# A two-block transformer kernel: gathered pairs in another order, three sets of expert weights, and tile 0's gated sum ahead of late dot products

## What is computed

```python
# block 1
mod = silu(c) @ w_ada + b_ada                  # six vectors of 1024
y = g_attn * (attn @ w_o_attn) + g_rec * (rec @ w_o_lru)      # the gated sum
x = x + gate1 * (y @ w_out)
h2 = rms_norm(x, norm2_g) * (1 + scale2) + shift2
q = (h2 @ w_query).reshape(tokens, 8 heads, 2, 128)
s = einsum('thpd,hpnd->thpn', q, sub_keys)     # two lists of 128 key scores
s_top, i_top = top_k(s, 16)                    # then the 16 best of 16 x 16 sums
idx, g = ...                                   # 16 experts of 16384 per token and head
act = gelu(einsum('td,thkd->thk', h2, expert_u[idx]))
x = x + gate2 * einsum('thk,thkd->td', g * act, expert_v[idx])
# block 2: attention and short convolution, then 32 experts with two chosen per token
hid = silu(xb @ w1[e]) * (xb @ w3[e]);  ys = hid @ w2[e]
```

## Time and profile before

| | |
|---|---|
| runs, us | 1626.86, 1626.68, 1625.25 |
| profiled execution, us | 1625.88 |
| its span, first to last instruction, us | 1624.0 |
| TensorE matmul busy | 1450.2 us, 89% of the span |
| TensorE weight loads | 1178.8 us, 73% |
| VectorE busy | 884.4 us, 54% |
| ScalarE busy | 485.5 us, 30% |
| GpSimd busy | 297.0 us, 18% |
| moved by DMA | 595.88 MB, mean 367 GB/s |

### The profile page before, as it was taken

The page is one execution under the profiler, slowest core; times in us unless marked ns, Lnnn a source line. Parts: engine busy times, 40 slices in busy tenths (PEclk is TensorE's granted clock), DMA queues, the critical chain, the costliest instruction groups (busy, mean ns, idle before and its releaser), DMA issues.

```text
span 1624.0 us, 25750 instructions
## 1 busy us (share of the span) xinstructions
PE 1450.2 (89%) x10126; PEld 1178.8 (73%) x10126; DVE 884.4 (54%) x2305; ACT 485.5 (30%) x1293; POOL 297.0 (18%) x277
## 2 busy tenths in 40 slices
PE   5999999998888888889888899999899998888887
PEld 4888999998888888888877747888755554444444
DVE  6788868787777777777775547612451211111112
ACT  2153312544444444444443412210321111111111
POOL 0000012344444444444445100000000000000000
PEclk9999999999999999999989999999899999999999
DMA  9665967999999999999999977564589999999997
GB/s 382 267 244 220 388 233 284 411 408 420 420 421 420 418 417 420 418 417 421 420 416 418 406 290 293 207 280 186 208 375 402 413 433 431 427 430 434 430 433 313
DMA packets 61152, 595.88 MB, mean 367 GB/s; under 512 B 6912, under 2 KB 7424, under 8 KB 13184
## 3 DMA queue, kind: packets, MB, share of 16 engines
q1 hardware_dynamic: 21744, 317.21, 47.2%
q0 software_dynamic: 39312, 277.37, 41.5%
HBM read 593.50 MB, written 1.05 MB: 366 GB/s over the span
## 4 chain that ended last, share of the span: by engine, by line
PE 54%; DMA 28%; DVE 12%; issue 2%; ACT 2%; SPq 0%; POOL 0%; DVEq 0%; POOLq 0%; ACTq 0%
PE bank L699 14%; DMA weight_slabs<-in_w_moe 14%; PE bank L1008 13%; DMA weight_slabs<-in_expert_uv,work 9%; PE bank L1178 5%; PE bank L1151 3%; PE bank L902 3%; DMA gathered_rows<-in_expert_uv,work 3%; PE bank L1062 3%; DMA weight_slabs<-in_slabs 2%; DVE weight_slabs L2058 2%; PE bank L1206 2%; DVE gathered_rows L2058 1%; PE bank L931 1%; DVE weight_slabs L1612 1%
## 5 line engine op out<-in xcount | busy, mean ns | idle before, releaser
L1008 PE MATMUL bank<-work,gathered_rows 128*128 128x128 f32 x2048 | 261.5, 286 | 46.4 <-ACT work L1448 46.4
L1008 PEld LDWEIGHTS bank<-work,gathered_rows 128*128 128x128 f32 x2048 | 254.6, 201 | 55.5 <-ACT work L1448 51.4
L1008 PE MATMUL bank<-work,weight_slabs 128*128 128x128 f32 x2048 | 257.6, 283 | 34.4 <-ACT work L1448 34.4
L1008 PEld LDWEIGHTS bank<-work,weight_slabs 128*128 128x128 f32 x2048 | 249.5, 199 | 42.7 <-ACT work L1448 40.8
L699 PE MATMUL bank<-hT,weight_slabs 128*128 128x256 f32 x928 | 205.0, 381 | 0.0
L2058 DVE CUSTOM_DVE_ANT_0 weight_slabs<-weight_slabs,work 128x1024 f32<-128x1024 f32 x128 | 155.5, 1225 | 79.7 <-DMA weight_slabs<-in_expert_uv,work 76.9
L2058 DVE CUSTOM_DVE_ANT_0 gathered_rows<-gathered_rows,work 128x1024 f32<-128x1024 f32 x128 | 155.4, 1224 | 79.0 <-DMA gathered_rows<-in_expert_uv,work 77.6
L699 PEld LDWEIGHTS bank<-hT,weight_slabs 128*128 128x128 f32 x928 | 176.3, 191 | 26.9 <-issue 3.1
L1543 POOL DMA_INDIRECT weight_slabs<-in_expert_uv,work x128 | 150.7, 1177 | 165.8 <-PE bank L1008 160.7
L1543 POOL DMA_INDIRECT gathered_rows<-in_expert_uv,work x128 | 136.9, 1070 | 213.8 <-PE bank L1008 177.6
L2266 DVE COPY work<-bank 128x512 f32<-128x512 f32 x32 | 22.1, 691 | 255.1 <-PE bank L1139 255.1
(11 more groups left out here) (376 smaller groups left out, 1734.1 us busy)
## 6 DMA issues: line engine op xcount, KB each, us to landing
weight_slabs<-in_w_moe SPq DMA_DIRECT2D x28, 4096.0 KB, 25.3
weight_slabs<-in_slabs SPq DMA_DIRECT2D x46, 2048.0 KB, 9.2
weight_slabs<-in_w_moe SPq DMA_DIRECT2D x34, 2048.0 KB, 21.9
weight_slabs<-in_slabs SPq DMA_DIRECT2D x16, 512.0 KB, 12.4
dots_ring<-in_slabs POOLq DMA_DIRECT2D x16, 512.0 KB, 7.4
gathered_rows<-in_w_moe SPq DMA_DIRECT2D x2, 2048.0 KB, 15.8
gathered_rows<-in_w_moe SPq DMA_DIRECT2D x1, 4096.0 KB, 19.7
weight_slabs<-in_slabs SPq DMA_DIRECT2D x2, 1024.0 KB, 15.0
```

What stands on the lines that cost most here:

```text
L1008: ins = nc.tensor.matmul(ps[2 * t + c // 4][:, (c % 4) * P:(c % 4 + 1) * P], row_at[k][:, D + c * P:D + (c + 1) * P], diag[:, k, :], start ...
```

## The change

Four edits. First, VectorE makes tile 0's gated sum after one dot product of ada11 instead of four and a ring dot; the ring dots that stood around it come behind `amuls`. TensorE does one piece less of chunk ylb0 before the wait for `y_ready` and the pieces of ylb0 and ylb1 move one place later. Second, the order of pairs is (0,0), (0,1), (0,2), (0,3), (1,0), (0,4), and so on; heads 2 and 3 of tile 0 get queries of their own (chunks pqf and pqg), tile 1's heads 2 and 3 get theirs later (pq12, pq13), and heads 4 to 7 are still made for both tiles. Third, tile 1's path moves from rows 0 to 16 to rows 14 to 45. Fourth, the expert stage has three whole sets of slots up to block 29: the ring becomes a w2 slot (block 2's w2 is loaded there right after w_o_21), the spread slot holds block 3's w2, and loads for block e wait for block e - 3. Blocks 30 and 31 and any more still go by the table with two sets.

```diff
+    pl += [("pqf", "A", []), ("scf", "A", []), ("pqg", "A", []), ("scg", "A", []), ("xb0", "D", ["w_out0"]), ("xb1", "D", ["w_out1"])]
+    SL += [("moe2_w2", SLAB), ("moe2_w1", SLAB)] + [...]
+    WEIGHT_SETS = [(m0, m1, m2), (m3, m4, m5), (NSLOT + 1, NSLOT, NSLOT + 3)]
+    PAIRS = [(0, 0), (0, 1), (0, 2), (0, 3), (1, 0), (0, 4), (1, 1), (0, 5), (1, 2), (0, 6), (1, 3), (1, 4), (1, 5), (1, 6), (0, 7), (1, 7)]
+    SINGLE = {2: ("pqf", "scf", 2, 0, 2), 9: ("pqg", "scg", 3, 0, 9), 39: ("pqe", ...), 82: ("pq12", ...), 116: ("pq13", ...)}
+    DOUBLE = [(4, 44, 2), (5, 60, 1), (6, 92, 1), (7, 130, 1)]
 # SyncE, expert stage
         sp.wait_ge(chunk_ready, INDEX["hu3"] + 1)
-        load_third(2)
+        load_spread(3)
+        for b in range(3, FIRST_BLOCKS):
+            sp.wait_ge(m_w13, b - 2)
+            load_pair(g["w13_moe"][b], b % 3)
+            if b > 3:
+                sp.wait_ge(m_w2, 2 * (b - 2))
+                load_last(g["w2_moe"][b], WEIGHT_SETS[b % 3][2])
+        with sp.Fori(1, STATIC_ROUNDS) as i:
+            for j in range(PER_ROUND):
+                e = i * PER_ROUND + j
+                sp.wait_ge(m_w13, i * PER_ROUND + (j - 2))
+                load_pair(...)
+                sp.wait_ge(m_w2, i * (2 * PER_ROUND) + 2 * (j - 2))
+                load_last(...)
 # TensorE
-        recurrent("ylb0", 0, 2)
+        recurrent("ylb0", 0, 1)
         pe.wait_ge(y_ready, 1)
 ...
-        pe.wait_ge(y_ready, 2)
-        done(out_features(begin("xb0"), 1, 0, 4))
-        begin("xb1")
 ...
+                for name, scored, h, t, first in SINGLE.values():
+                    if first <= n < first + 4:
+                        tile_query(name, h, t, 4 * (n - first), 4 * (n - first) + 4)
+                if 14 <= n < 30 and n % 2 == 0:
+                    d = (n - 14) // 2
+                    last = out_features(bank(f"xb{d // 4}"), 1, d, d + 1)
-                if n == 4:
+                if n == 32:
                     sum_tile(1)
-                if n == 8:
+                if n == 36:
                     tile_query("pqc", 0, 1)
 # VectorE
-        slab_dots("ada11")
-        ring_dots(1)
+        slab_dots("ada11", 0, 1)
         attended_part("a", 0, 0)
-        ring_dots(1)
+        slab_dots("ada11", 1, 3)
         attended_part("a", 0, 1)
         V.nop().then_inc(y_ready, 1)
+        slab_dots("ada11", 3, 4)
         mod_bias(0, 2)
         amuls(1, "norm2_g")
+        ring_dots(2)
 ...
-                if m == 0 and r == 3:
+                if m == 1 and r == 8:
                     residual_tile(1, 0)
-                if m == 0 and r == 5:
+                if m == 1 and r == 15:
                     residual_tile(1, 1)
-                if m == 0 and r == 10:
+                if m == 2 and r == 5:
                     norm_rest(1)
```

More of the change, by code:

```diff
@@ L225, in bank_plan @@
 def bank_plan(plan):
-    banks, turn = [], 2
+    banks, turn = [], 1
     split = {"yaa0": 4, "yaa1": 5, "xa0": 0, "xa1": 1, "ss2a": 7, "ylb0": 6, "pqa": 3, "pqb": 4, "sca": 5, "ht0": 6, "ht1": 7, "pqd": 3, "scd": 4,
-             "ylb1": 2, "yab0": 5, "yab1": 6, "xb0": 2, "xb1": 3, "ss2b": 7, "pqc": 4, "ht2": 6, "ht3": 7, "scc": 5, "pqe": 4, "sce": 5, "xq0": 0, "xq1": 1, "xr0": 2, "xr1": 3, "ss4a": 6, "ss4b": 7,
+             "ylb1": 2, "yab0": 5, "yab1": 6, "xb0": 2, "xb1": 3, "pqf": 7, "scf": 4, "pqg": 5, "scg": 6, "ss2b": 7, "pqc": 4, "ht2": 6, "ht3": 5, "scc": 7, "pqe": 4, "sce": 6, "xq0": 0, "xq1": 1, "xr0": 2, "xr1": 3, "ss4a": 6, "ss4b": 7,
              "ss3a": 4, "ss3b": 5, "zq0": 6, "zk0": 7, "zv0": 3, "zq1": 4, "zk1": 0, "zv1": 1}
@@ L917, in _ @@
             done(out_features(begin(f"xa{i}"), 0, 4 * i, 4 * i + 4))
-        recurrent("ylb0", 2, 3)
+        recurrent("ylb0", 1, 2)
         sum_tile(0)
-        done(recurrent("ylb0", 3, 4))
-        begin("ylb1")
-        recurrent("ylb1", 0, 1)
+        done(recurrent("ylb0", 2, 4))
         def query(h, a=0, z=2 * DC):
@@ L954, in _ @@
                     done(last)
-        recurrent("ylb1", 1, 2)
+        begin("ylb1")
+        recurrent("ylb1", 0, 1)
         first_keys = slab3(16, P)(slab("keys"))
@@ L976, in tile_query @@
                     pe.wait_ge(h_ready, H_BASE[1] + DC * t + k + 1)
[L977 to L978 removed]
+                f0 = T * (h % 2) + p * P
+                last = nc.tensor.matmul(b[:, p * P:(p + 1) * P], w[:, k, f0:f0 + P], hT[:, k, tile(t)], start=(k == 0), stop=(k == DC - 1))
             if z == 2 * DC:
```

196 lines of the change are left out of this document (105 added, 91 removed).

## The result

The changed kernel takes 1631.86 us, the median of 12 runs, against 1626.61 us for 12 runs of the kernel before beside it: ratio 1.0027, 95% interval 1.0016 to 1.0038, that is **4.4 us slower** (2.6 to 6.2); the medians alone lie 5.3 us apart. The forecast was 1620.2 us. The profiled execution took 1631.97 us, with a span of 1630.1 against 1624.0.

What follows compares the result with a forecast made beforehand. It took both long stages, gather and experts, to be bound by DMA bytes. +2.8 (gather's end) - 9.3 (experts) = -6.5 us took the profiled 1625.88 to 1619.4; the median, 0.8 higher, was 1620.2 us, range 1613.5 to 1628.

Steps and rivals of the forecast that it cites:

- Part 1, "-1.1": Tile 0's gated sum ahead of late dots: the first gather would be issued 1.1 us earlier, at 260.4.
- at 224.6 + 7.2 = 231.8: Fourth ring chunk, needed by the fifth ring dot: asked for at 224.6, it would land 7.2 us later.
- chunks late by one us more: Lower bound for tile 0's head start: 0 us if ring chunks landed one us later; 1.1 was taken.
- all the rest of tile 0's chain has the same instructions ... and shifts with it: Square to route 0 in tile 0 would keep its length, moving the first gather from 261.53 to 260.4.
- TensorE owes one piece more ... That costs nothing.: One 1.8 us piece behind the query makes ylb1 and yab1 0.7 us later, at no cost to the gather.
- Part 2, "+3.9 on the length of the gather": New pair order and tile 1's later path: 6.1 us of idle DMA in the gather against 2.2 before.
- Block 2 up to the experts ... shift as one.: Gather's end, its last two pairs and block 2 up to the experts would keep their length: change 0.
- Part 3, "-9.3": Expert stage with three sets: the last w2 would be in 9.3 us earlier, relative to the stage's start.
- 4.9 for the bytes and 4.3 for the gap: Expert stage: -4.9 us from 2 MB fewer remaining at 1181, -4.3 us from closing the gap at 1250 to 1260.
- Rival C: Expert stage: third set only moves gaps; only the 2 MB count, less the new gap; 1625.5 us, chance 0.14.
- The end, "0": From the last w1 and w3 issue through the last products and store to the end: no change forecast.
- Rival D: Gather: TensorE and VectorE become the bound of the first four pairs; slower, 1631 us, chance 0.11.

Runs made afterwards that it cites:

- e1: Kernel before with only tile 0's gated sum moved ahead of the late dots: +1.4 us against before (ratio 1.0009).
- e2: Kernel before with only the new order of pairs and tile 1's path moved to rows 14 to 45: +5.7 us against before (1.0035).
- e3: As e2, but tile 1's w_out and residual at their old place: +3.1 us against before (1.0019).
- e14: Changed kernel with four matmuls by zeros ahead of block 2's first scores: +1.8 us against before (1.0011).
- e4: Kernel before with only the three sets of expert weights, block 2's w2 in the ring: -8.2 us against before (0.9949).
- e9: As e4, but from block 6 on loads again wait for block e - 2: +2.1 us against before (1.0013).
- e5: Changed kernel without the gated sum moved ahead, so new pairs and three sets: +1.8 us against before (1.0011).
- e8: As e6, with four matmuls by zeros in the middle of tile 0's sum of squares: -6.0 us against before (0.9963).
- e13: Changed kernel unaltered, timed and profiled once more: +5.6 us against before (1.0034).
- e6: Kernel before with the gated sum moved ahead and three sets, without the new pairs: -8.4 us against before (0.9948).
- e7: As e6, but the two ring dots behind amuls moved behind route 0; reads overwritten numbers, serves for time alone: -5.0 us against before (0.9969).
- e10: Changed kernel with seven matmuls by zeros ahead of block 2's first scores: +2.4 us against before (1.0015).
- e15: As e4, with three matmuls by zeros ahead of block 2's first scores: -9.8 us against before (0.9940).
- e12: As e4, with seven matmuls by zeros ahead of block 2's first scores and three before each of the last two blocks' weights: -5.2 us against before (0.9968).

## Why the prediction was wrong

**What bounds the kernel** was right: both long stages end with their bytes. Most of what went wrong lies between them or at their ends, where I forecast zeros.

1. *Part 1, "-1.1".* xa0 started at 221.94 (forecast 221.75), and the fifth dot waited for its chunk. Measured +1.6 (+2.2 by the means over all traces); missed 2.7 us, by two steps that failed. The first is the landing, "at 224.6 + 7.2 = 231.8": asked for 0.7 us later and 1.0 us longer on its way, the chunk was in at 233.5, and the second residual half came at 240.86 (forecast 239.1), 0.66 later than in before. That is 1.8 of the 2.7 us, just beyond my bound of 0 for "chunks late by one us more". The second is "all the rest of tile 0's chain has the same instructions ... and shifts with it": the same matmuls took longer at the lower clock, about 1 us.
2. *"TensorE owes one piece more ... That costs nothing."* True while the slabs fill (e1, 661.5). With part 2 there is no filler, the piece is ahead of the first row dot, and it costs 1.8 us. I had costed each part against the kernel before and not against each other.
3. *Part 2, "+3.9 on the length of the gather"*: e2 +3.8. e3 confirms the reason. With point 2 it became +6.2.
4. *"Block 2 up to the experts ... shift as one."* They did up to the transposes, 74.79 us in both. Behind them stand 2.5 us, idle time and clock; e14 shows the clock's part. The idle time there is set by the landing of a slab, as the lines of VectorE above show. Why the slab lands later there is open.
5. *Part 3, "-9.3".* The stage gave 7.1 by the issues and 6.9 in e4. The gap was closed as forecast, and TensorE starved from about block 18 on (1420.20; forecast 19). Mis-sized was the idle time: I took 1613.3 as the end of the last w2, and the last bytes of before move at about 1611.1 (the windows of 1610 to 1616 have a share of 0.17). Of the 8.5 us 6.3 were there. Wrong too was the split into 4.9 for the bytes and 4.3 for the gap as two gains: e9 shows that the bytes ahead without the depth widen the gap. Rival C, by which the third set only moves gaps, is refuted by e4, for this stage.
6. *The end, "0".* It added 0.9, 1.7 and 1.7 us, the largest piece of the miss. The failed step is that the end was taken over from before without a wait or a clock of its own. The products are long by the clock: 5.2 to 5.3 us behind idle times of 2.54 to 2.94 us in after, e5, e8 and e13, 3.64 behind 1.6 us in all others without zeros there. The late landing came with them in these four, not in e4, e6, e7, e9, e10, e14 and e15, which have the same sets. More traffic isn't the reason: in the 24 us behind the issue after moved 10.18 MB and e10 10.27. What makes the landing late, and the store's 1.7 us, is open.

Rival D gave 1631 us and the sign that came, but not by its mechanism: by it the gather would end 13 to 16 us later, it ended 7.8 later, and from 340 to 880 every window of 60 us in after moves 415 to 420 GB/s, so TensorE and VectorE are no bound there. It was right by chance. What came instead were several waits and fallen clocks of 1 to 3 us, most of them outside the two stages that I had counted.

## What to carry to other kernels

Cost each part of a change against the others as well: filler that one part removes may be what made a second part free. Where an earlier result only lengthens an engine's wait ahead of the same late input, look at the clock of the matmuls behind the wait, and cover idle time with work that is shorter than it, measured first. Before a stretch of one trace is called an effect, compare all traces that have the same code there. Between load queues and a compute loop, depth (how many blocks ahead a load may go) and bytes already loaded are not two gains: without the depth, the bytes ahead only empty the queue sooner.

## What the runs showed of the hardware

- TensorE's granted clock fell behind single idle times of 2.5 to 4.2 us (0.76 over 7 us behind 3.58 of idleness; 0.63 and 0.69 over ten us behind 3.97). Such a wait cost 1.0 to 2.7 us in the matmuls behind it. The Trainium skill, "TensorE: Matmul & The Clock Gate", section "HAM oscillation — how this bites in real kernels", describes this for a loop that waits for its loads; the traces agree, and show it in single waits.
- Between 2.5 and 2.7 us it was not the same each time: it had fallen behind 2.54 us at the end of after and 2.55 at e12's last row, and not behind 2.54 and 2.61 at the last row of e4 and of after, nor behind 2.66 at e8's scores. It did not fall behind the waits of 1.6 us between the expert blocks.
- So stretches with the same code take one of two lengths. From the last row dot to the transposes it is 74.8 or 76.4 us, by the clock of the last row's matmuls (2.05 us, or 2.52 to 3.68) and of those behind them. From the hT load to load 3 it is 15.6 to 15.9 or 16.8 to 17.3 us (both in the changed kernel: 15.68 and 17.18), and the first expert block's 32 products, at a mean granted clock of 0.55 to 0.74, take 4.9 to 5.7 us in the short ones and 6.0 to 6.6 in the long. The last load takes 25.4 or 26.3 to 26.7 us and the store 5.2 or 6.9, and for these two no cause is shown. One profile of a stage of this kernel is good to about 1.5 us, no better.
- A matmul by zeros, 128 x 512 in float32, takes 0.88 us on TensorE (seven in 6.17 us).
